# Expert 30's second projection placed ahead of expert 31's first projection, in the epilogue of a mixture-of-experts loop

## The reference

```python
logits = xt @ w_router + b_router            # 256 tokens, 32 experts
top_vals, top_idx = lax.top_k(logits, 4)
gates = jax.nn.softmax(top_vals, axis=-1)
# for every expert e, on the tokens that chose it:
gu = xb @ w1[e] + b1[e]                      # w1[e]: 1024 x 2048, 8 MB
gate = jnp.minimum(gu[:, :F], 7.0)
up = jnp.clip(gu[:, F:], -7.0, 7.0)
act = (up + 1.0) * gate * jax.nn.sigmoid(1.702 * gate)
y = act @ w2[e] + b2[e]                      # w2[e]: 1024 x 1024, 4 MB
x = x + (y weighted by the gates, added back to the tokens)
out = rmsnorm(x, norm_final_g)
```

## Time and profile before

| | us |
|---|---|
| median of 3 runs | 1274.87 |
| lowest and highest | 1273.74 and 1274.90 |
| the profiled execution, its own time | 1276.97 |
| its span, first to last instruction | 1275.1 |
| TensorE busy | 1180.4 (93%) |
| VectorE busy | 364.3 (29%) |
| ScalarE busy | 216.3 (17%) |
| data moved by DMA | 462.37 MB |
| mean granted clock of TensorE, as a share of full speed | 0.992 |

### The profile page before, as it was taken

How to read it: one execution, slowest core, us unless ns; L and a number is a source line. 1 busy time by engine, 2 the same in 40 slices (tenths; PEclk the granted TensorE clock), 3 DMA queues, 4 the chain that set the end, 5 groups by cost and what they waited for, 6 DMA issues and landing times.

```text
span 1275.1 us, 17461 instructions
## 1 busy us (share of the span) xinstructions
PE 1180.4 (93%) x7307; PEld 604.6 (47%) x7307; DVE 364.3 (29%) x656; ACT 216.3 (17%) x325; POOL 57.2 (4%) x38
## 2 busy tenths in 40 slices
PE   5999999999799999999999988899999999989897
PEld 5999888998633333333333333333333333333332
DVE  4764754633522221121121111111211121111112
ACT  4444444431600000000000000000000000000001
POOL 0850000000300000000000000000000000000000
PEclk9999999999889999999999999999999999999999
DMA  9755435941699999999999999999999999999995
GB/s 309 235 189 192 157 139 205 368 155 72 257 427 426 428 428 429 430 428 429 429 428 428 429 428 429 429 428 428 430 428 428 428 428 429 429 429 428 430 427 233
DMA packets 56163, 462.37 MB, mean 363 GB/s; under 512 B 5578, under 2 KB 7171, under 8 KB 31587
## 3 DMA queue, kind: packets, MB, share of 16 engines
q1 hardware_dynamic: 52776, 458.58, 86.7%
q10 hardware_dynamic: 3354, 3.33, 0.8%
HBM read 460.82 MB, written 1.07 MB: 362 GB/s over the span
## 4 chain that ended last, share of the span: by engine, by line
PE 59%; DMA 38%; DVE 1%; ACT 1%; issue 0%; SPq 0%; DVEq 0%; ACTq 0%
DMA w_ring<-in_w 25%; PE ps L1052 16%; DMA behind_xb<-in_w 12%; PE ps L1102 11%; PE ps L852 4%; PE ps L854 4%; PE ps L855 4%; PE ps L1146 3%; PE ps L1042 2%; PE ps L980 2%; PE ps L859 2%; PE ps L861 2%; PE ps L860 2%; PE ps L975 1%; PE ps L1083 1%; DMA w_ring<-in_w_in 1%
## 5 line engine op out<-in xcount | busy, mean ns | idle before, releaser
L1052 PE MATMUL ps<-w_ring,A_W 128*64 128x512 f32 x1376 | 315.3, 603 | 41.2 <-DMA w_ring<-in_w 39.7
L1052 PEld LDWEIGHTS ps<-w_ring,A_W 128*64 128x64 f32 x1376 | 93.8, 138 | 236.7 <-issue 161.7
L1505 DVE TENSOR_SCALAR A_W<-ps 128x512 f32<-128x512 f32 x32 | 22.1, 692 | 507.9 <-PE ps L1052 507.9
L1102 PE MATMUL ps<-w_ring,A_W 128*64 128x512 f32 x688 | 156.0, 595 | 0.1
L1224 DVE TENSOR_TENSOR w_parts<-w_ring,w_parts 128x1024 fp32r<-128x1024 f32 x76 | 108.7, 1442 | 89.3 <-ACT w_parts L623 85.4
L852 PE MATMUL ps<-hT_hi,w_parts 128*128 128x256 f32 x384 | 110.3, 287 | 2.0 <-ACT hT_hi L642 2.0
L781 ACT ACTIVATE A_W<-A_W 128x512 f32<-128x512 f32 x32 | 20.2, 630 | 538.8 <-DVE A_W L1505 538.8
L854 PE MATMUL ps<-hT_lo,w_parts 128*128 128x256 f32 x384 | 109.8, 286 | 0.0
L855 PE MATMUL ps<-hT_hi,w_parts 128*128 128x256 f32 x384 | 109.7, 286 | 0.0
L623 ACT ACTIVATE w_parts<-w_ring 128x1024 fp32r<-128x1024 f32 x76 | 80.0, 1058 | 84.9 <-PE ps L855 54.4
L1052 PE MATMUL ps<-behind_xb,A_W 128*64 128x512 f32 x336 | 76.6, 598 | 9.9 <-DMA behind_xb<-in_w 9.9
(11 more groups left out here) (214 smaller groups left out, 1096.7 us busy)
## 6 DMA issues: line engine op xcount, KB each, us to landing
w_ring<-in_w SPq DMA_DIRECT2D x128, 2048.0 KB, 38.8
behind_merged<-in_w SPq DMA_DIRECT2D x21, 2048.0 KB, 38.8
behind_xb<-in_w SPq DMA_DIRECT2D x21, 2048.0 KB, 39.5
behind_gates<-in_w SPq DMA_DIRECT2D x21, 2048.0 KB, 37.9
w_ring<-in_w_in SPq DMA_DIRECT2D x38, 1024.0 KB, 7.2
w_ring<-in_w_ret_branch SPq DMA_DIRECT2D x2, 2048.0 KB, 13.3
A_W<-in_w_out SPq DMA_DIRECT2D x1, 2560.0 KB, 14.5
xb<-in_x SPq DMA_DIRECT2D x4, 512.0 KB, 3.7
```

The costliest lines, as they stand in the source:

```text
L1052: mm = pe.matmul(o, XT[:, k, :], tile[:, j, c * HALF:(c + 1) * HALF], start=(k == 0), stop=(k == KC - 1))
L1102: mm = pe.matmul(ps[CAP * c:CAP * c + CAP, 3, :], lhs, w2_tile(flat)[:, q % W2_ROWS, c * HALF:(c + 1) * HALF], start=False, stop=(q == FQ ...
```

## The change

In the epilogue both units of w2 of expert 30 are loaded and used ahead of the four units of w1 of expert 31. The two functions that number the units follow: w2 of expert 30 becomes 184 and 185, w1 of expert 31 becomes 186 to 189. In the order of TensorE the scatter of expert 29 and `project_down` of expert 30 come first, then `hidden` of expert 31, the scatter of expert 30, `transpose_act` and `project_down_last` of expert 31. A wait of TensorE on `swe` ahead of `transpose_act` falls away, as the scatter in front of it has the same wait. In the order of VectorE the stores of expert 30, and the slots for expert 31, come ahead of the activation of expert 31. ScalarE's program is not touched.

```diff
         def w1_number(e, u):
+            if e == N_EXP - 1:
+                return N_UNITS - E_UNITS + u
             return u if e == 0 else W1_UNITS + E_UNITS * (e - 1) + u
         def w2_number(e, u):
-            return W1_UNITS + E_UNITS * e + W1_UNITS + u if e < N_EXP - 1 else N_UNITS - W2_UNITS + u
+            if e >= N_EXP - 2:
+                return N_UNITS - W2_UNITS - E_UNITS * (N_EXP - 1 - e) + u
+            return W1_UNITS + E_UNITS * e + W1_UNITS + u
...
+            for u in range(W2_UNITS):
+                n = w2_number(N_EXP - 2, u)
+                sp.wait_ge(s_used, n - RING + 1)
+                load_w2(sp, N_EXP - 2, u, n)
             for u in range(W1_UNITS):
                 n = w1_number(N_EXP - 1, u)
                 sp.wait_ge(s_used, n - RING + 1)
                 load_w1(sp, N_EXP - 1, u, n)
-            for u in range(W2_UNITS):
-                n = w2_number(N_EXP - 2, u)
-                sp.wait_ge(s_used, n - RING + 1)
-                load_w2(sp, N_EXP - 2, u, n)
...
-            hidden(N_EXP - 1, w1_number(N_EXP - 1, 0))
             scatter(main, N_EXP - 2)
             project_down(N_EXP - 2, w2_number(N_EXP - 2, 0))
-            pe.wait_ge(main.swe, N_EXP)
+            hidden(N_EXP - 1, w1_number(N_EXP - 1, 0))
+            scatter(main, N_EXP - 1)
             transpose_act(main, N_EXP - 1)
-            scatter(main, N_EXP - 1)
             project_down_last(N_EXP - 1)
             scatter_last(main, N_EXP)
...
             gated_slots(main, N_EXP - 2, N_EXP - 2)
-            hidden_done(N_EXP - 1)
-            activate(main, N_EXP - 1)
             store_scatter(main, N_EXP - 2)
-            down_done(N_EXP - 2)
+            dve.wait_ge(s_used, w2_number(N_EXP - 2, W2_UNITS - 1) + 1)
             store_y(main, N_EXP - 2)
             choose_bias(sel2, main.sel2, N_EXP - 1)
             gated_slots(main, N_EXP - 1, N_EXP - 1)
+            dve.wait_ge(s_used, w1_number(N_EXP - 1, W1_UNITS - 1) + 1)
+            activate(main, N_EXP - 1)
             store_scatter(main, N_EXP - 1)
```

## The result

The changed kernel took 1278.41 us in the median of 6 runs (1277.76 to 1280.01), the kernel before 1274.88 us in the median of 6 (1272.40 to 1276.11). The ratio is 1.0032, with a 95% interval of 1.0019 to 1.0045. So the change made the kernel slower by some 3.5 us.

The account below looks back on a forecast made before the run. Transfers set the loop's pace; the end is set by unit 189's landing and TensorE's work behind it. Bare activation 1.9 plus clock fall 1.7 gave +3.6 us on 1274.87, so 1278.5 us, range 1276.0 to 1279.5.

Parts of the forecast that it names:

- bare activation: Behind unit 189, expert 31's activation is uncovered, so the last projection's bias starts 1.96 us later; +1.9 us used.
- Loads unchanged: Units 184 to 191 land when they did before, only their contents change; 0 us.
- third rival: w1 units come faster than w2 units, unit 189 lands 1.9 us earlier, time 1274.9 us or below; chance 0.04.
- TensorE makes up its lag ahead of unit 189: In the epilogue, idle times before w1 units absorb a lag of up to 1 us; 0 us.
- One fall of the clock: In the tail behind unit 189, TensorE's clock drops once to 1.2 GHz with matmuls uncovered; +1.7 us.
- That it falls: The clock falls in the new idle stretch behind unit 189, somewhat likelier than not; forecast with one fall has 0.50.
- first rival: The clock holds in the new stretch behind unit 189; +1.9 us, 1276.8 us, within 0.2%; chance 0.40.
- The reason for the fall: New tail has 2.2 us idle in 2.9 us; at the first expert 1.80 us idle were followed by a fall.

Follow-up runs that it names:

- b_gap: Kernel before with two more VectorE instructions ahead of the copy of expert 30's result, idling TensorE behind the transposes; timed, median 1276.69 us, ratio 1.0017.
- a_noact: Changed kernel without expert 31's activation, the transposes taking expert 30's activations; 14.78 us from unit 189's first matmul to the copy of the last result.
- a_fill_small: Changed kernel with two throw-away matmuls of 128x512 ahead of expert 31's transposes and two of 128x256 behind; median 1275.67 us, ratio 1.0008 against the kernel before.

## Why the prediction was right

The forecast was 1278.5 us, and 1278.41 was measured; the sum was +3.6 against +3.52 in D. The mechanism was right, the bare activation by its working and the fall by a judgement not much better than even. That the two times agree to 0.1 us is luck, given what the executions differ by. By its steps:

- **Loads unchanged.** Right. Units 188 and 189 are used 4.89 and 4.90 us apart, each after an idle time that ends on DMA, and in the second traces unit 189 starts at 1248.26 before and 1248.29 after. The third rival, a w1 unit that lands earlier than a w2 unit, has nothing for it.
- **TensorE makes up its lag ahead of unit 189.** Right. w2 of expert 30 was to end 13.9 us ahead of unit 189 and ended 14.0 ahead (1234.34); the wait for unit 187 is 0.18 us, for 188 and 189 the full 1.24.
- **Bare activation, +1.96, taken as +1.9.** Right in place and size: 8.30 us to the bias against 6.37, D +1.95.
- **One fall of the clock, +1.7.** It measured 1.57. The size came from 16 matmuls with one fall at the first expert. There all of it lay on matmuls; in the trace after the clock was at 0.50 already at 1256.5, while TensorE still waited for the bias (1256.65).
- **That it falls.** I called this somewhat likelier than not and gave the forecast 0.50 and the holding clock 0.40. It came in 14 of 21 executions, by the mean clocks. The first rival, +1.9, was what the other 7 did by the same measure, so the two were not two outcomes but a mixture in one kernel. The five traces without a fall at the first expert show that it was a mixture there too. The Trainium skill, "TensorE: Matmul & The Clock Gate", Part 1, has it that the place of the change differs from run to run, and here the traces agree: three of four without a fall, one with it. The Trainium skill, same page, section "Why this matters for your kernels", warns only of longer idle gaps; had shorter ones been harmless, the sum would have been +1.9, and the measured medians and the first trace speak against that.
- **The reason for the fall** was right in kind but too simple. I went by the 1.80 us of idle time at the first expert, and `b_gap` shows 1.40 us behind transposes going without. With both idle stretches filled, the times show no executions with a fall. Why the fall comes in some executions and not in others stays open. `a_noact` has the second stretch alone, in one trace without a fall; the first alone wasn't tried.
- **Not in the prediction:** the last stretch, 2.67 to 4.90 us over all traces and not bound to the kernel. It and the stages ahead of the loop differ by up to 2.2 and 3.2 us between the traces. The four traces of the changed kernel have 3.8 to 4.05 and the two of the kernel before 4.12 and 2.75, too few to say whether the change has a part in it. Together with the times of `b_gap_timed` and `a_fill_small`, which D doesn't account for by 1.0 us up and 1.5 us down, this means that the median says less than D on what the change is worth. The split into 1.95 and 1.57 rests on the traces.

## What to carry to other kernels

At the end of a kernel bound by transfers, list what has to follow the last unit of each kind, and put last the weights with the least behind them: w1 of the last expert draws an activation and a transpose behind it, while w2 needs only a copy and a scatter. When two traces are compared, take the distance between two events inside the changed stage and not the span, and when a tail is bare, ask of every new wait in it what TensorE's clock does afterwards, since here 2 us of waiting cost 1.57 us more in one trace of four and, by the means and times, in two executions of three. And a single trace in which the clock fell or held behind a short wait shows one outcome of several: look at more than one before a forecast rests on it.

## What the runs showed of the hardware that was not expected

- One program, D of 17.72 and of 16.15 us: with 1.29 and 0.78 us of idle time around four transposes, the granted clock went to 0.50 for some 3 us in one trace and not in three others. With 1.40 us in one piece behind the transposes it didn't in two.
- The same 1.80 us of idle time at the first expert, ahead of the same work, was followed by a fall in nine traces (16 matmuls in 5.35 us) and not in five (3.65 us).
- Four throw-away matmuls in the idle time (1.5 us of TensorE's time) cost nothing in D (16.18 against 16.15). The trace had 1.00 throughout, and none of 11 executions had the time of one with a fall.
- The four output stores and what follows them take between 2.7 and 4.9 us behind the last instruction of the norm. SP's issue of the four lasted 3.54 us in the first trace of before and 2.50 us in its second. What goes with it can be read from the DMA view of a run from 1 us ahead of the end of the chain to 2 us behind it. In the ten traces with a last stretch of 3.84 us or more one transfer of instructions (queue q8) starts there, in the four with 2.67 to 2.75 none does. For the trace after, over 1269.50 to 1276.70:

```profile
q1 hardware_dynamic: 576, 1.05, 39.5%
q8 instruction: 1, 0.02, 0.9%
```

That is 14 of 14, but it goes together only; no run moved the transfer by itself.
